# State space chunks prepared two ahead, ScalarE's order turned, squares added on GpSimd, and wide final sums

## The reference

```python
# state space branch, chunk by chunk, for each of 8 groups of 4 heads
acum = jnp.cumsum(ac, axis=1)
seg = acum[:, :, None] - acum[:, None, :]
decay = jnp.exp(jnp.where(causal, seg, -jnp.inf))
cb = jnp.einsum("blgn,bsgn->blsg", cc, bc)
y = jnp.einsum("blsgr,bsgrp->blgrp", cb[..., None] * decay, xc)
y = y + jnp.einsum("blgn,bgrpn->blgrp", cc, h) * jnp.exp(acum)[..., None]
h = jnp.exp(acum[:, -1])[..., None, None] * h + jnp.einsum("blgn,blgrp->bgrpn", bc, to_end[..., None] * xc)
...
# then, per group of 256 channels
y = y * silu(z)
y = y * lax.rsqrt(jnp.mean(y * y, axis=-1, keepdims=True) + EPS) * norm_g
...
# the branch gates, from the same projection
gates = h @ w_in[:, OFF_GATE:]
...
# at the very end
y = x * lax.rsqrt(jnp.mean(x * x, axis=-1, keepdims=True) + EPS) * final_g
```

## Time and profile before

| | us |
|---|---|
| median of three runs | 5069.1 |
| the profiled execution | 5071.81 |
| its span in the trace | 5070.0 |
| state space stage, first to last TensorE record | 920.4 to 1630.5 |
| one group, by the starts of their first transposes (1264.92 to 1352.92) | 88.0 |
| final stage, from the first squares' sum to the end | 5014.3 to 5070.0 |
| TensorE busy / VectorE / ScalarE / GpSimd, share of the span | 91 / 70 / 36 / 30 % |

### The profile page before, as it was taken

The page is one execution under the profiler, slowest core; times in us unless marked ns, Lnnn a source line. Parts: engine busy times, 40 slices in busy tenths (PEclk is TensorE's granted clock), DMA queues, the critical chain, the costliest instruction groups (busy, mean ns, idle before and its releaser), DMA issues. The chain is left out here.

```text
span 5070.0 us, 83754 instructions
## 1 busy us (share of the span) xinstructions
PE 4601.9 (91%) x28889; PEld 4277.1 (84%) x28889; DVE 3568.5 (70%) x6872; ACT 1803.2 (36%) x3737; POOL 1496.6 (30%) x1358
## 2 busy tenths in 40 slices
PE   7999999688887989997988578999999999999997
PEld 5999999677776659896887567999999999999997
DVE  3101555454554652344899997999999999999996
ACT  3111333232322552223444693333333333333332
POOL 0000000111110000000000004777777777777773
PEclk9999999888888779997999799999999999999997
DMA  4332222223232324433999358999999999999996
GB/s 158 120 134 90 83 88 95 110 98 108 102 110 83 70 60 155 181 131 124 355 335 337 148 198 324 372 363 367 373 366 381 377 370 367 378 374 370 380 377 222
DMA packets 350790, 1170.27 MB, mean 231 GB/s; under 512 B 40128, under 2 KB 91456, under 8 KB 344256
## 3 DMA queue, kind: packets, MB, share of 16 engines
q0 software_dynamic: 147456, 536.94, 28.2%
q1 hardware_dynamic: 160480, 483.07, 26.5%
q10 hardware_dynamic: 42720, 148.52, 7.7%
HBM read 971.20 MB, written 197.46 MB: 231 GB/s over the span
## 5 line engine op out<-in xcount | busy, mean ns | idle before, releaser
L2198 POOL DMA_INDIRECT ex_vr<-in_expert_v,ex_at x512 | 610.9, 1193 | 225.9 <-issue 152.9
L2196 POOL DMA_INDIRECT ex_ur<-scr_u_rows,ex_at x512 | 573.6, 1120 | 296.6 <-issue 118.1
L2385 DVE SCALAR_TENSOR_TENSOR ex_acc_rows<-ex_vr,ex_wt,ex_acc_rows 128x1024 f32<-128x1024 f32 x512 | 648.7, 1277 | 1.0 <-DMA ex_vr<-in_expert_v,ex_at 0.6
L2377 DVE SCALAR_TENSOR_TENSOR ex_ur<-ex_ur,h_rows 128x1024 f32<-128x1024 f32 x512 | 615.3, 1216 | 21.5 <-DMA ex_ur<-scr_u_rows,ex_at 20.6
L2190 POOL COPY ex_at<-picked_at 128x4 uint32 x128 | 103.1, 805 | 1494.8 <-POOLq L125 1494.3
L933 POOL TENSOR_TENSOR sd_cts<-sd_cT,sd_ea 128x512 f32<-128x512 f32 x72 | 92.5, 1284 | 1427.6 <-ACT sd_ea L891 1427.6
L2208 PE MATMUL ex_ps<-hd_hi,ex_u_hi 128*128 128x320 f32 x2048 | 469.3, 310 | 18.2 <-PEq L125 16.4
L2208 PE MATMUL ex_ps<-hd_lo,ex_u_hi 128*128 128x320 f32 x2048 | 469.2, 310 | 0.0
L2208 PE MATMUL ex_ps<-hd_hi,ex_u_lo 128*128 128x320 f32 x2048 | 468.4, 310 | 0.0
L2299 ACT ACTIVATE ex_gel<-ex_dot 128x1 f32<-128x1 f32 x512 | 103.7, 203 | 903.5 <-DVE ex_ur L2377 903.5
L479 DVE TENSOR_TENSOR pr_w_lo<-pr_w,pr_w_hi 128x1024 fp32r<-128x1024 f32 x56 | 68.6, 1225 | 488.0 <-ACT pr_w_hi L475 488.0
(11 more groups left out here) (359 smaller groups left out, 11386.4 us busy)
## 6 DMA issues: line engine op xcount, KB each, us to landing
pk_raw_u<-in_expert_u SPq DMA_DIRECT2D x128, 512.0 KB, 6.5
scr_u_rows<-pk_rows_u ACTq DMA_DIRECT2D x128, 512.0 KB, 6.2
ex_u<-in_expert_u SPq DMA_DIRECT2D x128, 512.0 KB, 6.7
ex_v<-in_expert_v SPq DMA_DIRECT2D x128, 512.0 KB, 8.4
scr_gate<-gt_stage SPq DMA_DIRECT2D x10, 4096.0 KB, 12.6
ex_gate<-scr_gate SPq DMA_DIRECT2D x32, 1280.0 KB, 8.9
pr_w<-in_w_main SPq DMA_DIRECT2D x58, 512.0 KB, 4.6
scr_xbc<-pr_out ACTq DMA_DIRECT2D x32, 576.0 KB, 3.7
```

Of the source, the lines that this page charges most:

```text
L2196: nc.gpsimd.indirect_dma_start(out=ur[:, s], out_offset=None, in_=scr["u_rows"], in_offset=by).then_inc(ur_in[s], 16)
L2198: nc.gpsimd.indirect_dma_start(out=vr[:, s], out_offset=None, in_=io["expert_v"].rearrange("j i d -> (j i) d"), in_offset=by).then_inc(vr_ ...
L2377: v.scalar_tensor_tensor(out=ur[:, s], in0=ur[:, s], scalar=1.0, in1=rows[:, s], op0=ALU.mult, op1=ALU.mult, accum_out=dot[:, m:m + 1]).th ...
L2385: v.scalar_tensor_tensor(out=acc_g[:, s], in0=vr[:, s], scalar=wt[:, m:m + 1], in1=acc_g[:, s], op0=ALU.mult, op1=ALU.add).then_inc(row_r[ ...
```

## The change

1. Chunks are prepared two ahead instead of one, and `psA` gets a second buffer. Its PSUM bank comes from `psR`, which has one buffer now; so each of the eight sample rows and each piece of `spread` waits for VectorE to have read the one before.
2. In a chunk TensorE's gate products stand ahead of `prepare`, not behind it; there are 9 in each of chunks 1 to 8 (72 of 144) where 8 stood in each of chunks 1 to 6 (48 of 144). Each sample row is followed by 9 where 12 were.
3. ScalarE takes `ea` and `dec` of a chunk first and copies `bk` then.
4. VectorE: `masked(c+1)`, then the state, then `before(c+2)`, then y's output.
5. GpSimd adds the two halves of a group's squares, and `variances` takes 9 products (18 records) for 18 (36).
6. The three pieces of `spread` stand after chunks 3, 5 and 6, which were 3, 3 and 4.
7. In `finish_output` the squares are summed by products with a matrix of ones as the stationary operand and 512, 512 and 128 columns; the sums lie in all partitions at once. Root and reciprocal are taken of 128 x 1152, and nothing is spread.

```diff
-        psA = pb("sd_psA", [P, 512])
+        psA = pb("sd_psA", [P, 2, 512])
...
-        psR = pb("sd_psR", [P, 2, 512])
+        psR = pb("sd_psR", [P, 512])
...
-        SPREAD = {3: (0, 2), 4: (2, NV)}
-        USED = {3: 0, 4: 1, 5: 2}
+        SPREAD = {3: (0, 1), 5: (1, 2), 6: (2, NV)}
+        USED = {3: 0, 5: 1, 6: 2}
         TAKEN = {4: 0, 7: 1}
-        IN_CHUNK = 8
-        IN_CHUNKS = IN_CHUNK * (LAST - 2)
+
+        IN_CHUNK = 9
+        IN_CHUNKS = IN_CHUNK * LAST
...
-                    if n == 0:
+                    if b == 0:
                         pe.wait_ge(used_r, (i * 2 + s) * NV + START)
-                    pe.wait_ge(sb_done[e], (i * 2 + s) * SEMS_OF[e] + n + START)
-                    last = mm(psR[:, e, 0:W], bk[:, q], xeb[:, e], start=True, stop=True)
+                    else:
+                        pe.wait_ge(sb_done[1 - e], (i * 2 + s) * SEMS_OF[1 - e] + (b - 1) // 2 + 1 + START)
+                    last = mm(psR[:, 0:W], bk[:, q], xeb[:, e], start=True, stop=True)
...
-                pe.wait_ge(sq_r, i * 2 + s + 1 + START)
+                pe.wait_ge(both_r, i * 2 + s + 1 + START)
...
                 for c in range(NT):
-                    for j in range(2):
-                        last = mm(psR[:, 0, c:c + 1], sq[:, j, c * P:(c + 1) * P], ones[:, 0:1], start=(j == 0), stop=(j == 1))
+                    last = mm(psR[:, c:c + 1], sq[:, 0, c * P:(c + 1) * P], ones[:, 0:1], start=True, stop=True)
...
             def group(i, s, before):
+
                 prepare(i, s, 0)
+                prepare(i, s, 1)
                 for c in range(NT):
-                    if c < LAST:
-                        prepare(i, s, c + 1)
-                        if 0 < c < LAST - 1:
-                            gates(i, s, (c - 1) * IN_CHUNK, c * IN_CHUNK)
+                    if c > 0:
+                        gates(i, s, (c - 1) * IN_CHUNK, c * IN_CHUNK)
+                    if c + 2 <= LAST:
+                        prepare(i, s, c + 2)
                     scan(i, s, c)
...
+            def add_squares(g):
+                pool.wait_ge(sq_r, g + 1 + START)
+                nc.gpsimd.tensor_tensor(sq[:, 0], sq[:, 0], sq[:, 1], ALU.add).then_inc(both_r, 1)
...
                 before(0)
+                before(1)
                 masked(0)
                 for c in range(NT):
                     if c < LAST:
-                        before(c + 1)
-                    after(c)
+                        masked(c + 1)
+                    if 0 < c < LAST:
+                        state(c)
+                    if c + 2 <= LAST:
+                        before(c + 2)
                     if c < LAST:
-                        masked(c + 1)
+                        output(c)
+                    else:
+                        sample_states()
+                    if c == 0:
+                        state(0)
...
-            v.reciprocal(rs[:], rs[:]).then_inc(rec_r, 1)
-            dve.wait_ge(spread_r, 1 + START)
+            v.reciprocal(rstd[:], rstd[:]).then_inc(rec_r, 1)
+            dve.wait_ge(rec_r, 1 + START)
...
-            nc.scalar.activation(rs[:], vps[:, 0:NT], ACT.Sqrt, bias=per["eps"][:, 0:1], scale=1.0 / D).then_inc(rooted, 1)
+            nc.scalar.activation(rstd[:], ps[:, 0:T], ACT.Sqrt, bias=per["eps"][:, 0:1], scale=1.0 / D).then_inc(rooted, 1)
...
-                for t in range(NT):
-                    last = nc.tensor.matmul(vps[:, t:t + 1], sq[:, k % 2, t * P:(t + 1) * P], ones[:, 0:1],
-                                            start=(k == 0 and t == 0), stop=(k == KD - 1 and t == NT - 1), skip_group_check=True)
+                for a, n in COLS:
+                    last = nc.tensor.matmul(ps[:, a:a + n], ones, sq[:, k % 2, a:a + n], start=(k == 0), stop=(k == KD - 1))
```

More of the change, by code:

```diff
@@ L826, in spread @@
                     a, w = COLS[n]
[L827 to L828 removed]
+                    if n > 0:
+                        pe.wait_ge(used_r, g * NV + n + START)
                     for t in range(w // P):
[L830 removed]
+                        last = mm(psR[:, t * P:(t + 1) * P], rs[:, a // P + t:a // P + t + 1].to_broadcast([P, P]), ident, start=True, stop=True)
                     last.then_inc(spread_r, 1)
@@ L855, in roots @@
                 act.wait_ge(spread_r, g * NV + START)
-                nc.scalar.activation(rs[:], psR[:, 0, 0:NT], ACT.Sqrt, bias=per["eps"][:, 0:1], scale=1.0 / W).then_inc(root_r, 1)
+                nc.scalar.activation(rs[:], psR[:, 0:NT], ACT.Sqrt, bias=per["eps"][:, 0:1], scale=1.0 / W).then_inc(root_r, 1)
             def round_gate_weights(i, s, j, first):
@@ L882, in group @@
                     u = i * (CH // 2) + u
+                    act.wait_ge(cum[q], u + 1 + START)
+                    act.wait_ge(cts_r[q], u + START)
+                    act.wait_ge(h_done[q], u + START)
+                    act.wait_ge(seg_r[q], u + 1 + START)
+                    nc.scalar.activation(ea[:, q].rearrange("p r l -> p (r l)"), psA[:, q], ACT.Exp).then_inc(ea_r[q], 1)
+                    act.wait_ge(mt_r[q], u + START)
+                    for r in range(R):
+                        last = nc.scalar.activation(dec[:, q, r], seg[:, q, r], ACT.Exp, bias=vg[:, s, 1, c, r:r + 1])
+                    last.then_inc(dec_r[q], 1)
                     act.wait_ge(tr[q], u + 1 + START)
@@ L886, in group @@
                     nc.scalar.copy(bk[:, q], psT[:, q, 2 * P:3 * P]).then_inc(bk_r[q], 1)
[L887 to L895, removed]
                     if c == 2:
@@ L996, in masked, with output @@
                     v.tensor_tensor(mt[:, q], dec[:, q], psT[:, q, 3 * P:4 * P].unsqueeze(1).to_broadcast([P, R, P]), ALU.mult).then_inc(mt_r[q], 1)
-                def after(c):
+                def output(c):
                     q, u, ms, at = chunk(s, c)
@@ L1008, in after, with state @@
                     ins.then_inc(y_read[q], 1)
+                def state(c):
+                    q, u, ms, at = chunk(s, c)
+                    u = i * (CH // 2) + u
+                    dve.wait_ge(y_r[q], u + 1 + START)
+                    dve.wait_ge(s_r[q], u + 1 + START)
                     if c == 0:
@@ new lines, in sample_states, with rows_of, update @@
+                def sample_states():
+                    q, u, ms, at = chunk(s, LAST)
+                    u = i * (CH // 2) + u
+                    dve.wait_ge(xdt_r[q], u + 1 + START)
+                    dve.wait_ge(h_in, g * 16 + 16 + START)
+                    def rows_of(b):
+                        e, n = b % 2, b // 2
+                        dve.wait_ge(sb_r[e], g * SEMS_OF[e] + n + START)
+                        v.tensor_scalar(xeb[:, e], xe[:, q], per["const"][:, C_BM + b:C_BM + b + 1], None, ALU.mult).then_inc(xeb_r[e], 1)
+                    def update(b):
+                        e, n = b % 2, b // 2
+                        hv = h0[:, b].rearrange("p (r d) -> p r d", d=HD)
+                        ch.link(v.tensor_tensor(hv, hv, ea[:, q, :, b * TS + TS - 1:(b + 1) * TS].to_broadcast([P, R, HD]), ALU.mult))
+                        if b < NB - 1:
+                            dve.wait_ge(sb_r[e], g * SEMS_OF[e] + n + 1 + START)
+                        else:
+                            dve.wait_ge(s_r[q], u + 1 + START)
+                        v.tensor_tensor(h0[:, b], h0[:, b], psR[:, 0:W], ALU.add).then_inc(h_done[q] if b == NB - 1 else sb_done[e], 1)
+                    rows_of(0)
+                    output(LAST)
+                    for b in range(NB):
+                        if b < NB - 1:
+                            rows_of(b + 1)
+                        update(b)
```

49 lines of the change are left out of this document (12 added, 37 removed).

## The result

| | before | after |
|---|---|---|
| median, us | 5069.1 | 5080.25 |
| range of nine runs | 5064.07 to 5079.8 | 5074.08 to 5085.31 |
| the profiled execution and its span | 5071.81, 5070.0 | 5078.99, 5076.9 |

The ratio is 1.0021, with a 95% interval of 1.0012 to 1.003: the change made the kernel 11 us slower. I had forecast 6.4 us faster (5062.7 on the scale of the medians).

The account below looks back on a forecast made before the run. TensorE was taken to bound the state space stage. That stage's +2.6 and the final stage's -9.0 us gave -6.4, from 5071.8 to 5065.4, or 5062.7 on the median's scale; own range 5045 to 5080, of all 5017 to 5097.

Parts of the forecast that it names:

- the final stage: After the last group: wide sums end 13.4 us earlier, root and reciprocal add 4.4; together -9.0 us.
- The single pauses: TensorE's waits in a state space group under the new order, laid out one by one; with +1.3 for results, 15.9 us.
- weights: Chunk 1's gate products wait for VectorE, which rounds their weights only after output(0) and state(0): 1.1 us a group.
- 25th product: In chunk 3, this gate product waits for ScalarE's first result copy, queued behind its chunk 4: 4.2 us a group.
- 49th: This gate product waits likewise for ScalarE's copy behind its chunk 7, which hangs on scan(5): 2.6 us a group.
- last y: The last chunk's y waits as its exponential is queued behind store_y, which waits for normalize: 1.6 us, 3.12 before.
- group end: At the group's end 9 gate products instead of 12 cover VectorE's product of y and z: 2.4 us, 1.72 before.
- two results in the rows: Two gate results end within the sample rows, each costing TensorE 0.65 us: 1.3 us a group.
- So +1.0: State space stage, per group: new pauses of 15.9 us against old ones of 14.9, raised from 12.4 for overlap.
- The clock term: Low-clock loss a state space group: 6.4 us before, 8.3 after, so +1.9; called the weakest term.
- The variances' 18 records: TensorE's variances in a group take 18 records for 36, 2.0 us instead of 4.9: -2.9 us.
- Rival 2: Waits at the 25th and 49th gate product each bring a low-clock stretch of 6.8 us: +37, 5099 us; chance 0.22.

Follow-up runs that it names:

- kernel 2: The changed kernel with the old final stage, so only the state space stage's changes; ratio to the kernel before 1.0027.
- kernel 1: The kernel before with only the new final stage (wide sums, root and reciprocal of 128x1152); state space stage unchanged; ratio to the kernel before 0.998.
- kernel 3: The changed kernel with 8 gate products a chunk instead of 9; ratio to the kernel before 0.9886.
- Kernels 9 and 10: Each is kernel 4 with one reordering undone: gate products behind the preparation again (0.9762), or ScalarE's copy of B ahead of the exponentials again (0.98).
- kernel 4: kernel 3 with ScalarE's store of y behind its last chunk and the first gate weights rounded right behind masked(0); ratio to the kernel before 0.9745.
- kernel 6: kernel 3 with only the early rounding of the first gate weights, right behind masked(0); ratio to the kernel before 0.9838.
- kernel 7: kernel 4 with 9 gate products a chunk instead of 8; ratio to the kernel before 0.9908.
- kernel 5: kernel 3 with only ScalarE's store of y moved behind its work in the last chunk; ratio to the kernel before 0.9796.
- kernels 8: kernel 4 without GpSimd's sum of squares, so TensorE takes 36 narrow records for 18; ratio to the kernel before 0.9802.

## Why the prediction was wrong

In one sentence: the final stage came as forecast, each pause of the state space stage did too, but the sum of the new pauses was set against a sum of the old ones that had been raised by a correction, and so the cost of the reordering was put at 1.0 us a group where it is 3.0.

**The final stage was right.** The sums take 22.7 us (5029.57 to 5052.23) instead of 35.4: -12.7, forecast -13.4. The first tile starts at the lower clock and takes 5.0 from start to start, the second 2.9, and then they are 2.5 apart; the clock's record is at 1.00 from 5035.5. At the full clock a tile's sums keep TensorE 1.94 to 2.04, from their start to the start of what follows, where 1.95 was forecast. Root 1.22 (forecast 1.3), reciprocal 7.35 (7.4), tail +4.3 (+4.4). The slope of the earlier trace rows held at sixteen times the larger of its two sizes. The estimate from the repeat count of 8 in the Trainium skill (VectorE: DVE Perf Modes, "the 8-slice pipeline in each mode") and the 0.96 GHz of its page "SBUF — State Buffer" ("SBUF: two separate sides") was 9.6 us. The trace does not agree with it: 7353 ns for 1152 elements are 6.4 ns an element, not 8.3.

**The single pauses were right.** Forecast pause and measured idle time a group: chunk 2 behind `masked(0)` 2.7 and 2.7 (16.0 / 6); weights 1.1 and 0.9; 25th product 4.2 and 3.7; 49th 2.6 and 3.0; last y 1.6 and 1.9; group end 2.4 and 1.9 ((6.2 + 5.0) / 6); two results in the rows 1.3 and 1.2. The sum is 15.9 forecast and 15.3 measured.

**The step that failed is the subtraction behind "So +1.0".** I set 15.9 against 14.9, having raised the measured 12.4 by 0.25 for each of ten pauses, "by which the last record overlaps". But the overlap is about 0.15 where I could check it: the preparation of chunk 1 begins at 1184.23 and takes 1.47, and chunk 2's starts at 1188.34, 2.64 later, where the idle reads 2.50. The 384-column records, 0.34 long with the next one 0.17 later, say nearly the same. With 0.15, before is 12.3 + 1.5 and after, with eight pauses, 15.3 + 1.2: +2.7 a group. By idle times alone, without any correction, it is +3.0, against either trace of the old code (12.3 in both). The correction was too large for the old pauses (0.25 for 0.15). And the pauses laid out for the new order, which were meant as start to start, came out as idle times (15.9 for 15.3) and not as times from start to start (16.5). A correction on one side only hid two thirds of what the reordering costs. Two us a group are 16 in eight groups; the stage was missed by 16.8 in this pair of traces, and by 11 by the ratio of kernel 2.

**The clock term was too low on both sides; whether its difference was wrong stays open.** Against work of 63.9 us at the full clock (65.8 with 18 records more), TensorE lost 10.1 a group before and 10.4 after; I had 6.4 and 8.3. So +0.3 instead of +1.9. But in kernel 1's trace the old code lost only 8.8, which makes it +1.6, close to the forecast. The variances' 18 records gave 1.9, not 2.9. Busy time: forecast -2.9 + 1.9 = -1.0, measured -1.6, or -0.3 against kernel 1's trace; the forecast lies between.

In the pair of before and after, a group is +3.0 - 1.6 = +1.4, forecast 0.0; six of them +8.5. The first group is 5.6 longer (forecast 1.3): its waits sum to 13.3 where they were 10.3, without the wait for the first data that both have, and its low time rose from 27 to 34. In kernel 2's trace the same first group is 2.7 shorter, with 24 of low time. From the last group's start to the product of y and z it is +2.9 (forecast 0), and behind that +2.4 (1.3). There TensorE waits 6.33 for GpSimd's sum where it waited 3.30 for the squares (+3.0, forecast +2.6), and its 18 records take 4.00 at the lower clock where 36 took 7.10 (-3.1, forecast -3.6).

**Rival 2 had the place but not the price.** Waits at the 25th and 49th product did decide the sign, as kernel 3 shows. In most groups a low stretch of 3.4 us follows each of them, not of 6.8. That low stretches elsewhere would shrink was right: in the group's second half one of 6.8 stands where one of 10.2 or 13.7 stood. "Nine instead of eight" I had taken as fixed, and costed its waits; I never asked what the same change would be worth at eight. Alone, this number turns +0.2% into -1.1%.

**Where the intended gain went.** Kernel 11 is the kernel before with the part on GpSimd alone; its group takes 83.5. With the reordering of the chunks on top, nine products in each, a group takes 89.6: the reordering costs 6 a group in the traces, and 5.6 by the ratios of kernels 2 and 11 (45 us in eight groups). With eight products it gains 2.8 (80.7 against 83.5), and with the two waits gone as well 12.3. Kernels 9 and 10 undo two parts of the reordering; no run undoes the others alone, so what the two chunks ahead or VectorE's new order give by themselves isn't shown.

What stays open is why a given pause is followed by low time in one group and not in the next of the same kernel: the six groups of kernel 4 have idle times of 5.8 to 6.3 us, and one with 5.9 has no low stretch where the five others have one of 3.4. Nor do the same waits give the same low time from one trace to the next: 21.0 a group in the kernel before, 18.2 in kernel 1.

## What to carry to other kernels

Compare idle time with idle time: a correction for how records overlap belongs on both sides or on neither. When work of one engine is cut into pieces as cover for others, let the pieces end where the other engine's buffer comes free. Nine products for eight cost 8.9 us a group, since the third and the sixth piece then reached over the end of a result, and the buffer for the next was not free yet. Where a TensorE stage shows low stretches, a pause can cost more than its length. Here the factor ran from 1.2 (kernel 6: 0.9 less idle, 1.1 a group) over 1.8 (kernel 7: 6.7 cost 11.8) to 3 (kernel 5: 2.29 cost 6.8), and no rule for it came out. And before a difference of two traces is split into terms, take a second trace of the same code: here it moved a group by 1.3 us, nearly as much as the change did (1.4).

## What the runs showed of the hardware

- With the same 521 records, TensorE's busy time in a group runs from 63.9 us at a granted clock of 1.00 (kernel 4) to 76.3 at 0.85 (after, 1271.57 to 1363.08). A pause of 2.0 to 2.3 us before records of 16 columns was followed by 10.2 us or more at 0.50 in each of six groups (kernel 3); without the pause the same records ran at 1.00 (kernel 5).
- Two traces of the same code, with waits that agree within 0.1 us a group, had 21.0 (before) and 18.2 us (kernel 1) at 0.50 in a group.
- 36 records of one column instead of 18 came with 6.3 us more of low time a group, with otherwise the same pauses (kernels 8 and 4: idle 5.9 and 6.0).
- A reciprocal on VectorE took 7.35 us for 1152 elements a partition, 6.4 ns each, and 604 ns for 72. An ordinary operation on the large tile took 1.42 us, a fifth of that.
- GpSimd's sum of two 128 x 1152 tiles took 2.63 us, as its rate on 1024 elements gave (2342 ns x 1152/1024).
